# Two matmuls on the same high weights made one of 512 columns, in a split-precision block of two transformer layers

## The chip, the cores and the metric

The kernel runs on one core of a Trainium2 chip. The metric is the device time of one execution in microseconds (us), lower is better. Engines are called by their names in the profile: PE is TensorE (matmuls), PEld its weight loads, DVE VectorE, ACT ScalarE, POOL GpSimd, SP the engine that issues most DMAs.

## The reference

The input is a sequence of 256 tokens with 2048 channels in f32. Two blocks follow one another. The first: an RMS norm, one input projection, sliding-window attention with sinks, a state-space branch (convolution of four taps, chunked scan), gates, an output projection, a gated feed-forward layer with 5632 hidden channels and a gated side input. The second: a norm, sparse attention in three branches, a convolution of 31 taps, an output projection and a feed-forward layer whose hidden channels pass through a convolution of three taps. Nearly all work is dense projections; cut to its core:

```
proj = rmsnorm(h) @ w_in                              # 2048 x 10784
h = h + merged @ w_o                                  # 2048 x 2048
h = h + (silu(f @ w_gate) * (f @ w_up)) @ w_down      # 2048 x 5632, twice, and 5632 x 2048
...
u = causal_depthwise_conv_2(h @ w_up_2, cw, cb)       # 2048 x 11264
a, gate = split(u)
x = x + (silu(gate) * a) @ w_down_2                   # 5632 x 2048
```

## The kernel before

Activations are held transposed: 128 channels on the partitions, the 256 tokens along the row. Weights stream in from memory once. Both are f32, and each is split in two parts of the rounded matmul type (fp32r): a high part, rounded, and a low part, the difference. A product then is three matmuls: high weights with high activations, high weights with low activations, low weights with high activations. The text calls these three a triple.

The work is a list of **units** (`all_units`). A unit makes 256 output channels, as two halves `m` of 128, from `nk` tiles of 128 input channels (16 as a rule, 22 for the down projections, 8 for `w_attn_br` and `w_out_2`). Its result fills one of PSUM's eight banks, 256 tokens for each half. A unit's weights come in pieces (`subs`) of up to four k-tiles x 256 channels, 512 KB. For each piece SP fetches it into one of four buffers `RAW` (as soon as the low split of the piece that had the buffer is done), ACT writes the rounded copy `wh` (one of five buffers, free when the matmuls five pieces ago are done), DVE writes `wl = raw - wh`, and PE multiplies. `make_plan` lays down one order of steps for all engines: the splits run four pieces ahead of the matmuls (`LEAD`); after a unit's last piece its end (`evac`, functions `ev_...`) is put in, and side work (attention, convolutions, the state-space scan, sums of squares for the norms) is put in by lanes, a step after each piece. Each engine carries out its steps strictly in that order, with semaphores between engines.

At a unit's end DVE reads the bank and scales it by the norm's root (`rb`), or adds it to the residual `H` (`ev_h`, `ev_fin`); then ACT and DVE do what the layer asks for. `ev_g2` and `ev_u2`, for example, run a convolution of three taps: two ACT instructions for the first tap, four of DVE for the others. The bank goes back to PE when the first DVE instruction has read it (`EMPTIED`, `bank_free`). Units take banks in turn out of (0, 1, 2), or out of `wide`, banks 0 to 4, in the feed-forward layers; side work uses the others.

A unit in which activations are the stationary operand (`nat`: `ev_v`, `ev_dt`, `ev_gate`, `ev_v2`) has the same three products with roles changed. High and low activations of a k-tile lie side by side in one row of 512 (`Acts.hi` and `Acts.lo`).

Of the kernel before, what the change touches and what calls it, by code (L numbers as in the profile page):

```python
# [15 lines left out]
P = 128  # L16
# [85 lines left out]
class Unit:  # L102
    def __init__(self, w, row0, nk, c0, rhs, ev, i, nc=256, nat=False, gens=(), gens2=(), before=(), mid=(),
                 banks=(0, 1, 2), pace=1, hold=0, k0=0):
        self.w, self.row0, self.nk, self.c0, self.rhs, self.ev, self.i = w, row0, nk, c0, rhs, ev, i
        self.nc, self.nat, self.gens, self.gens2 = nc, nat, list(gens), list(gens2)
        self.before, self.mid, self.banks, self.pace, self.hold, self.k0 = before, mid, banks, pace, hold, k0
# [10 lines left out]
def all_units():  # L118
    us = []
    add = lambda *p, **k: us.append(Unit(*p, **k))  # L120
    for i in range(4):
        add("w_in", 0, 16, 256 * i, "U1", "ev_q", i, mid=(("norm", 0, 0),) if i == 0 else (), hold=2 if i == 0 else 0,
            gens=([stage("rotary", 0, 3), stage("biases", 0, 2)] if i == 0 else []) + [stage("rope_q", i, 2)])
    add("w_in", 0, 16, 1024, "U1", "ev_k", 0, gens=[stage("rope_k", 0, 2), stage("rope_k", 1, 2)])
# [3 lines left out]
    for i in range(12):  # L128
        add("w_in", 0, 16, 3584 + 256 * i, "U1", "ev_xbc", i, gens2=[stage("conv4", i, 3)])
    for i in range(8):  # L130
        add("w_in", 0, 16, 6688 + 256 * i, "U1", "ev_ga", i, before=("all",) if i == 0 else (),
            gens=[stage("ssd", g, 6) for g in range(4)] if i == 0 else (), pace=2)
        add("w_attn_br", 0, 8, 256 * i, "AT", "ev_oa", i, pace=2)
    for i in range(8):
        add("w_in", 0, 16, 1536 + 256 * i, "U1", "ev_z", i, before=("side",) if i == 0 else ())
    for i in range(8):
        add("w_in", 0, 16, 8736 + 256 * i, "U1", "ev_gs", i, mid=(("norm", 1, 0),) if i == 0 else (),
            hold=HOLD if i == 0 else 0)
    for i in range(8):
        add("w_ssd_br", 0, 16, 256 * i, "YH", "ev_os", i)  # L140
    for i in range(8):
        add("w_o", 0, 16, 256 * i, "MH", "ev_h", i)
    wide = (0, 1, 2, 3, 4)
    for half in range(2):
        for i in range(11):
            first = half == 0 and i == 0
            add("w_gate", 0, 16, 256 * (11 * half + i), "F1", "ev_g1", 11 * half + i, banks=wide,
                mid=(("norm", 2, 0),) if first else (), hold=HOLD if first else 0)
            add("w_up", 0, 16, 256 * (11 * half + i), "F1", "ev_u1", 11 * half + i, banks=wide)
        for i in range(8):  # L150
# [4 lines left out]
            add("w_down", 2816 * half, 22, 256 * i, "G1", "ev_h", 8 + 8 * half + i, banks=wide, k0=22 * half)  # L155
    for i in range(8):
        add("w_ple_gate", 0, 16, 256 * i, "P1H", "ev_pg", i, mid=(("norm", 3, 0),) if i == 0 else (),
# [32 lines left out]
    for i in range(8):  # L190
        add("w_out_2", 0, 8, 256 * i, "MXA", "ev_h", 24 + i, before=("side",) if i == 0 else ())
    for half in range(2):
        for i in range(11):
            first = half == 0 and i == 0
            add("w_up_2", 0, 16, FFN + 256 * (11 * half + i), "F2", "ev_g2", 11 * half + i, banks=wide,
                mid=(("norm", 5, 0),) if first else (), hold=HOLD if first else 0)
            add("w_up_2", 0, 16, 256 * (11 * half + i), "F2", "ev_u2", 11 * half + i, banks=wide)
        for i in range(8):
            add("w_down_2", 2816 * half, 22, 256 * i, "G2", "ev_h" if not half else "ev_fin",
                32 + i if not half else i, banks=wide, k0=22 * half)  # L200
    return us


def make_plan(us):


    plan, subs = [], []
    side, conv = Lane(plan), Lane(plan)
    for n, u in enumerate(us):
        k = 0  # L210
        while k < u.nk:
            subs.append((n, k, min(NSUB, u.nk - k)))
            k += NSUB
    turns, gb = [], 0
# [9 lines left out]
    for s, (n, k, c) in enumerate(subs):  # L224
# [10 lines left out]
        if k == 0:  # L235
# [10 lines left out]
            u.bank = u.banks[gb % len(u.banks)]  # L246
            gb += 1
        plan.append(("sub", s, 0))
        if k + c == u.nk:
# [27 lines left out]
def hybrid_block_kernel(nc, a, out):  # L277
    units = all_units()
    plan, subs = make_plan(units)

# [115 lines left out]

    def f32(ap):
# [53 lines left out]

    A = {"U1": Acts("u1", AHt, 0), "AT": Acts("at", BIGt, 0), "YH": Acts("yh", BIGt, 0), "MH": Acts("mh", AHt, 0),
# [10 lines left out]
    rk_pe, rk_d = steps("rope_k_pe"), steps("rope_k_d", "x", "y", "kd")  # L463
    evq_d, evk_d, evv_a = steps("ev_q"), steps("ev_k"), steps("ev_v", "c0", "c1")
# [17 lines left out]
    h_d = steps("h_added")  # L482
# [21 lines left out]
    for c in range(9):  # L504
# [13 lines left out]
    fin_d, res_d = steps("fin_added"), steps("result")  # L518


    EMPTIED = {"ev_q": (evq_d, None), "ev_k": (evk_d, None), "ev_v": (evv_a, "c1"), "ev_dt": (dt_d, "x1"),
               "ev_xbc": (evx_d, None), "ev_ga": (ga_d, None), "ev_oa": (oa_d, None), "ev_z": (z_d, "z"),
               "ev_gs": (gs_d, None), "ev_os": (os_d, "a"), "ev_h": (h_d, None), "ev_g1": (g1_d, "z"),
               "ev_u1": (u1_d, "u"), "ev_pp": (pp_a, None), "ev_pg": (pg_d, "a"), "ev_ca": (ca_d, None),
               "ev_cg": (cg_d, "a"), "ev_cmp": (cmp_d, "k"), "ev_k2": (k2_d, None), "ev_v2": (v2_a, "c1"),
               "ev_gate": (gt_d, "c1"), "ev_q2": (q2_d, None), "ev_add": (add_d, None), "ev_g2": (g2_d, "z"),
               "ev_u2": (u2_d, "z"), "ev_fin": (fin_d, None)}
# [1788 lines left out]
```

## Time and profile before

| | |
|---|---|
| median of 3 runs | 3062.24 us (3054.26 to 3065.12) |
| profiled execution | 3059.82 us, span 3058.0 us |
| mean granted clock of TensorE | 0.965 of full |
| PE busy | 2920.3 us (95%), 23840 matmuls and as many loads |
| DVE busy | 1892.8 us (62%) |
| ACT busy | 1345.3 us (44%) |
| read from memory | 489.56 MB, 161 GB/s over the span |

The span runs from the first to the last instruction of the profiled execution. Matmuls overlap in the pipeline, so the mean length of one (about 0.28 us) says little; what counts is the distance from one start to the next. In the timeline, neighbours of one kind are merged into one row with their count.

### The profile page before, as it was taken

How to read it: one execution, taken by the hardware profiler on the slowest of the kernel's cores; microseconds unless marked ns; L12 is line 12 of the kernel's file. 1: busy time of each engine (PE TensorE's matmuls, PEld its weight loads, DVE VectorE, ACT ScalarE, POOL GpSimd, SP SyncE). 2: the span in 40 equal slices, each digit the busy share in tenths (PEclk: the TensorE clock that was granted, in tenths of full speed). 3: DMA queues.
4: the chain of work that ended last, by engine and by line, in shares of the span. 5: the costliest groups of instructions: out<-in, count | busy, mean ns of one | idle time of the engine just before them, and what ended most of it. 6: DMA issues, size and time to landing. Idle time of an engine off the chain costs nothing.

```text
span 3058.0 us, 55192 instructions
## 1 busy us (share of the span) xinstructions
PE 2920.3 (95%) x23840; PEld 2874.3 (94%) x23840; DVE 1892.8 (62%) x2677; ACT 1345.3 (44%) x1922; POOL 9.8 (0%) x19
## 2 busy tenths in 40 slices
PE   7988998999999999999999989986999999999998
PEld 7978998999999999999999989975889999999998
DVE  5556755756665554555555747867667775477754
ACT  4245444543444443344444632344555444355442
POOL 0000000000000000000000000000000000000000
PEclk8999999999999999999999988887999999999998
DMA  6434553565556665666556464432345555655554
GB/s 198 122 98 123 166 152 111 183 181 185 182 174 188 184 183 178 186 187 185 180 180 194 155 173 123 138 97 62 102 141 172 186 180 183 189 180 179 188 181 128
DMA packets 495006, 495.26 MB, mean 162 GB/s; under 512 B 19818, under 2 KB 493371, under 8 KB 494731
## 3 DMA queue, kind: packets, MB, share of 16 engines
q1 hardware_dynamic: 491424, 484.11, 51.9%
q0 software_dynamic: 1376, 5.05, 0.6%
q8 instruction: 187, 3.06, 0.4%
q10 hardware_dynamic: 1964, 2.58, 0.2%
q14 instruction: 55, 0.45, 0.0%
HBM read 489.56 MB, written 2.12 MB: 161 GB/s over the span
## 4 chain that ended last, share of the span: by engine, by line
PE 83%; DVE 9%; ACT 4%; issue 2%; DMA 1%; SPq 0%; DVEq 0%; ACTq 0%
PE PS L615 82%; DVE wl L1439 3%; DVE CC L1447 2%; ACT wh L1004 1%; DMA raw<-in_w_in 1%; ACT SX2a L1004 1%; ACT SX2b L1004 1%; DVE TA L1447 0%; DVE SQA L1439 0%; ACT SX1b L1004 0%; ACT SX1a L1004 0%; DVE H L1447 0%; DVE TC L1447 0%; ACT TB L1004 0%; DVE Z L1439 0%
## 5 line engine op out<-in xcount | busy, mean ns | idle before, releaser
L1439 DVE TENSOR_TENSOR wl<-raw,wh 128x1024 fp32r<-128x1024 f32 (+2 forms) x944 | 1109.5, 1194 | 790.4 <-ACT wh L1004 789.8
L1004 ACT ACTIVATE wh<-raw 128x1024 fp32r<-128x1024 f32 (+2 forms) x944 | 953.5, 1029 | 818.0 <-PE PS L615 792.1
L615 PE MATMUL PS<-CHt,wh 128*128 128x256 f32 x5632 | 1014.2, 283 | 0.0
L615 PEld LDWEIGHTS PS<-CHt,wh 128*128 128x128 f32 x5632 | 878.6, 192 | 0.0
L615 PE MATMUL PS<-BIGt,wh 128*128 128x256 f32 x4608 | 851.1, 287 | 1.4 <-DVE TA L1439 0.9
L615 PE MATMUL PS<-CHt,wl 128*128 128x256 f32 x2816 | 796.9, 283 | 0.0
L615 PE MATMUL PS<-AHt,wh 128*128 128x256 f32 x4160 | 771.9, 288 | 23.2 <-DVE wl L1439 15.9
L615 PEld LDWEIGHTS PS<-BIGt,wh 128*128 128x128 f32 x4608 | 731.8, 195 | 8.4 <-issue 5.5
L615 PEld LDWEIGHTS PS<-AHt,wh 128*128 128x128 f32 x4160 | 660.8, 195 | 33.2 <-issue 17.7
L615 PE MATMUL PS<-BIGt,wl 128*128 128x256 f32 x2304 | 658.5, 286 | 0.0
L615 PE MATMUL PS<-AHt,wl 128*128 128x256 f32 x2080 | 594.7, 286 | 0.0
L615 PEld LDWEIGHTS PS<-CHt,wl 128*128 128x128 f32 x2816 | 540.7, 192 | 0.0
L615 PEld LDWEIGHTS PS<-BIGt,wl 128*128 128x128 f32 x2304 | 449.6, 195 | 0.0
L615 PEld LDWEIGHTS PS<-AHt,wl 128*128 128x128 f32 x2080 | 406.0, 195 | 0.0
L1447 DVE SCALAR_TENSOR_TENSOR CC<-Z,CV,CC 128x256 f32<-128x256 f32 x240 | 99.7, 482 | 0.0
L1439 DVE TENSOR_TENSOR Z<-PS,RB 128x512 f32<-128x512 f32 x86 | 59.4, 691 | 41.5 <-PE PS L615 41.4
L1004 ACT ACTIVATE BIGt<-TC 128x256 fp32r<-128x256 f32 x88 | 31.9, 409 | 120.3 <-DVE TC L1439 120.3
L1447 DVE SCALAR_TENSOR_TENSOR TA<-Z,CV,TA 128x256 f32<-128x256 f32 x160 | 69.2, 482 | 15.0 <-ACT TA L1004 14.7
L1004 ACT ACTIVATE TB<-TA 128x512 f32<-128x512 f32 x34 | 21.5, 631 | 78.5 <-DVE TA L1447 78.5
L1004 ACT ACTIVATE SX2a<-SX2a,SM 128x128 f32<-128x128 f32 x64 | 26.1, 443 | 60.0 <-DVE SM L2068 52.4
L1004 ACT ACTIVATE TA<-Z 128x512 f32<-128x512 f32 x30 | 19.0, 632 | 75.2 <-DVE Z L1439 75.2
L1439 DVE TENSOR_TENSOR H<-H,PS 128x512 f32<-128x512 f32 x56 | 38.3, 684 | 18.3 <-PE PS L615 18.2
(269 smaller groups left out, 1562.4 us busy)
## 6 DMA issues: line engine op xcount, KB each, us to landing
raw<-in_w_up SPq DMA_DIRECT2D x264, 512.0 KB, 4.5
raw<-in_w_in SPq DMA_DIRECT2D x240, 512.0 KB, 3.7
raw<-in_w_down SPq DMA_DIRECT2D x160, 512.0 KB, 3.7
raw<-in_w_gate SPq DMA_DIRECT2D x88, 512.0 KB, 4.6
raw<-in_w_ssd_br SPq DMA_DIRECT2D x32, 512.0 KB, 4.6
raw<-in_w_o SPq DMA_DIRECT2D x32, 512.0 KB, 4.6
raw<-in_w_ple_gate SPq DMA_DIRECT2D x32, 512.0 KB, 4.5
raw<-in_w_out SPq DMA_DIRECT2D x32, 512.0 KB, 3.6
```

Of the source, the lines that this page charges most:

```text
L615: return e.matmul(o, l, r, start=start, stop=stop, skip_group_check=True)
L1004: return e.activation(o, x, f, **k)
L1439: return e.tensor_tensor(o, x, y, op)
L1447: return e.scalar_tensor_tensor(out=o, in0=x, scalar=s, in1=y, op0=o0, op1=o1)
```

## The change

Units get a mode. "one" is as before. In the two new modes, "joint" and "turn", each half `m` of the unit gets a whole bank of its own: one matmul multiplies the high weights with the 512 columns of high and low activations (`both`) into the bank, another multiplies the low weights with the high activations into the bank's first 256 columns. The first 256 columns, the near half, then hold two of the three products, the last 256, the far half, the third. The two are added at the unit's end: ACT copies the far halves into the place of the result (`far_half`), DVE adds the near ones there (`join_halves`), and what followed reads that place instead of the bank. `ev_h` and `ev_fin` add near and far half to `H` one after the other.

A "joint" unit goes through its pieces as before; a "turn" unit does the whole of one half before the other, in pieces of eight k-tiles x 128 channels. The weights are laid out in memory beforehand by piece (`_stream`), so that each partition reads one run of 4 KB for a piece and not four of 1 KB. The changed units from `ev_z` on take banks 0 to 3, the earlier ones stay with 0 to 2. A pair of banks is returned to PE when `joined` says so.

These keep mode "one": the units with stationary activations, `ev_pp`, the 16 units of `w_in_2` with the activations U2, and the 8 of the second block's convolution half (`ev_add`, activations MXC).

```diff
+    order = lambda i: "turn" if i else "joint"
+    wide = (0, 1, 2, 3)
...
-        add("w_ssd_br", 0, 16, 256 * i, "YH", "ev_os", i)
+        add("w_ssd_br", 0, 16, 256 * i, "YH", "ev_os", i, mode=order(i), banks=wide)
...
+def pieces(us):
+    subs, gb, joins = [], 0, 0
+    for n, u in enumerate(us):
+        if u.mode != "one" and len(u.banks) % 2 == 0:
+            gb += gb % 2
+        b = u.banks[gb % len(u.banks)]
+        gb += 1
+        u.bank, u.turn = b, (0, 1)
+        if u.mode != "one":
+            b2 = u.banks[gb % len(u.banks)]
+            gb += 1
+            u.turn = (0, 1) if b < b2 else (1, 0)
+            u.pair = (min(b, b2), max(b, b2))
...
+        for ms in (((u.turn[0],), (u.turn[1],)) if u.mode == "turn" else ((0, 1),)):
+            step = NSUB * 2 // len(ms)
+            subs += [(n, ms, k, min(step, u.nk - k)) for k in range(0, u.nk, step)]
+    return subs
...
-            src = a[u.w][r0:r0 + c * P, u.c0:u.c0 + u.nc].rearrange("(t p) n -> p t n", p=P)
+            src = a[units[subs[s][0]].w][w_at[s]:w_at[s] + P * w].rearrange("(p f) -> p f", p=P)
...
+                if u.mode != "one":
+                    for j, m in enumerate(ms):
+                        o = PS[:, u.pair[m], :]
+                        mm(o, hi[:, t, j * P:(j + 1) * P], x.both(kt), firstk, False)
+                        tok = mm(o[:, 0:T], lo[:, t, j * P:(j + 1) * P], x.hi(kt), False, lastk)
...
+        def far_half(u, o):
+            e.wait_ge(sub_done.sem, u.end)
+            for m, x in far(u):
+                tok = af(o[:, m], x, ACT.Copy)
+            tok.then_inc(far_out.sem)
...
+        def join_halves(u, o):
+            e.wait_ge(far_out.sem, far_out.at(u.join))
+            for m, x in near(u):
+                tok = tt(o[:, m], x, o[:, m], ADD)
+            tok.then_inc(joined.sem)
+            e.wait_ge(joined.sem, joined.at(u.join))
...
         def ev_g2(n, u):
-            e.wait_ge(sub_done.sem, u.end)
-            tt(Z[0][:, :, 30:286], bank(u.bank), two(rb(0)), MUL).then_inc(g2_d.sem)
+            join_halves(u, z)
+            tt(z, z, two(rb(0)), MUL).then_inc(g2_d.sem)
...
-            tt(h, h, bank(u.bank), ADD).then_inc(h_d.sem)
+            tt(h, h, near(u)[0][1], ADD).then_inc(h_d.sem)
+            e.wait_ge(h_d.sem, h_d.at(i, "near"))
+            tt(h, h, far(u)[0][1], ADD).then_inc(h_d.sem)
```

`near(u)` and `far(u)` give both banks in one view where they are neighbours, and two views, one for each half, where they are not (0 and 2).

## Rows read from the trace of the kernel before

**Rows 1.** The page: engines' busy time (share) and instructions, the chain's costliest line

```profile
PE 2920.3 (95%) x23840; PEld 2874.3 (94%) x23840; DVE 1892.8 (62%) x2677; ACT 1345.3 (44%) x1922; POOL 9.8 (0%) x19
...
PE PS L615 82%; DVE wl L1439 3%; DVE CC L1447 2%; ACT wh L1004 1%; DMA raw<-in_w_in 1%; ACT SX2a L1004 1%; ACT SX2b L1004 1%; DVE TA L1447 0%; DVE SQA L1439 0%; ACT SX1b L1004 0%; ACT SX1a L1004 0%; DVE H L1447 0%; DVE TC L1447 0%; ACT TB L1004 0%; DVE Z L1439 0%
```

**Rows 2.** Stretches: length, busy us of each engine (instructions), clock, DMA share, GB/s

```profile
517.40:1761.20 1243.80, 1241.09 (x10309) 1240.40 (x10308) 726.68 (x799) 549.65 (x670) 2.05 (x4) 1.00 0.59 180
1761.20:2278.10 516.90, 447.36 (x3496) 421.91 (x3497) 356.41 (x749) 215.43 (x417) 6.10 (x8) 0.87 0.40 116
2278.10:2533.30 255.20, 255.20 (x2126) 255.10 (x2126) 181.85 (x241) 128.62 (x167) 0.00 (x0) 1.00 0.58 182
```

**Rows 3.** Waits of PE: us in total, times, longest

```profile
PE PS L742 <- ACT SX1a L1004: 15.0, 4, 5.6
...
PE PS L615 <- DVE SQA L1439: 9.9, 2, 7.6
```

**Rows 4.** Timeline of PE, dense stretch: start us, length us, instruction, count

```profile
1004.87 0.28 PE L615 MATMUL PS<-CHt,wl 128*128 128x256 f32 x1
...
1005.23 0.28 PE L615 MATMUL PS<-CHt,wl 128*128 128x256 f32 x1
```

**Rows 5.** The page's costliest groups: the low-weight matmuls, one for each triple

```profile
L615 PE MATMUL PS<-CHt,wl 128*128 128x256 f32 x2816 | 796.9, 283 | 0.0
...
L615 PE MATMUL PS<-BIGt,wl 128*128 128x256 f32 x2304 | 658.5, 286 | 0.0
L615 PE MATMUL PS<-AHt,wl 128*128 128x256 f32 x2080 | 594.7, 286 | 0.0
```

**Rows 6.** Timeline of PE, 32-column matmuls of ev_dt, at two clocks

```profile
109.01 0.26 PE L615 MATMUL PS<-wl,AHt 128*128 128x32 f32 x1
...
109.34 0.26 PE L615 MATMUL PS<-wl,AHt 128*128 128x32 f32 x1
...
118.07 0.59 PE L615 MATMUL PS<-wh,AHt 128*128 128x32 f32 x2
...
118.71 0.59 PE L615 MATMUL PS<-wh,AHt 128*128 128x32 f32 x2
```

**Rows 7.** Timeline of PE's weight loads, 512-column f32 matmuls

```profile
1805.98 0.19 PEld L615 LDWEIGHTS PS<-BMR,M 128*128 128x128 f32 x1 [0.24 <-issue]
...
1807.27 0.19 PEld L615 LDWEIGHTS PS<-BIGt,wh 128*128 128x128 f32 x1 [0.24 <-issue]
```

**Rows 8.** Timeline of PE, the first triples after other work

```profile
355.21 0.28 PE L615 MATMUL PS<-AHt,wl 128*128 128x256 f32 x1
...
356.04 0.40 PE L615 MATMUL PS<-AHt,wh 128*128 128x256 f32 x2
```

**Rows 9.** Groups by form: evacuations like the added ones (busy us, mean ns)

```profile
L1439 DVE TENSOR_TENSOR Z<-PS,RB 128x512 f32<-128x512 f32 x86 | 59.4, 691 | 41.5 <-PE PS L615 41.4
...
L1004 ACT ACTIVATE PR<-PS 128x512 f32<-128x512 f32 x8 | 4.7, 583 | 0.0
```

**Rows 10.** Timeline of DVE over two units, ev_u2 and then ev_g2

```profile
2372.33 0.69 DVE L1439 TENSOR_TENSOR Z<-PS,RB 128x512 f32<-128x512 f32 x1 [0.57 <-PE PS L615]
2373.69 1.77 DVE L1447 SCALAR_TENSOR_TENSOR TC<-Z,CV,TC 128x256 f32<-128x256 f32 x4 [0.67 <-ACT TC L1004]
2375.57 0.69 DVE L1439 TENSOR_TENSOR TC<-TC,TA 128x512 f32<-128x512 f32 x1
...
2378.01 3.50 DVE L1439 TENSOR_TENSOR wl<-raw,wh 128x1024 fp32r<-128x1024 f32 x3 [0.50 <-ACT wh L1004]
2382.05 1.23 DVE L1439 TENSOR_TENSOR wl<-raw,wh 128x1024 fp32r<-128x1024 f32 x1 [0.55 <-ACT wh L1004]
2383.85 0.69 DVE L1439 TENSOR_TENSOR Z<-PS,RB 128x512 f32<-128x512 f32 x1 [0.57 <-PE PS L615]
...
2388.63 3.50 DVE L1439 TENSOR_TENSOR wl<-raw,wh 128x1024 fp32r<-128x1024 f32 x3 [0.26 <-ACT wh L1004]
```

**Rows 11.** The page's DMA issues: count, KB each, median us to landing

```profile
raw<-in_w_up SPq DMA_DIRECT2D x264, 512.0 KB, 4.5
```

More of the change, by code:

```diff
@@ L190, in all_units @@
     for i in range(8):
-        add("w_out_2", 0, 8, 256 * i, "MXA", "ev_h", 24 + i, before=("side",) if i == 0 else ())
+        add("w_out_2", 0, 8, 256 * i, "MXA", "ev_h", 24 + i, mode="turn", banks=wide, before=("side",) if i == 0 else ())
     for half in range(2):
@@ L194, in all_units, with weight_places @@
             first = half == 0 and i == 0
-            add("w_up_2", 0, 16, FFN + 256 * (11 * half + i), "F2", "ev_g2", 11 * half + i, banks=wide,
+            add("w_up_2", 0, 16, FFN + 256 * (11 * half + i), "F2", "ev_g2", 11 * half + i, banks=wide, mode=order(11 * half + i),
                 mid=(("norm", 5, 0),) if first else (), hold=HOLD if first else 0)
-            add("w_up_2", 0, 16, 256 * (11 * half + i), "F2", "ev_u2", 11 * half + i, banks=wide)
+            add("w_up_2", 0, 16, 256 * (11 * half + i), "F2", "ev_u2", 11 * half + i, banks=wide, mode="turn")
         for i in range(8):
             add("w_down_2", 2816 * half, 22, 256 * i, "G2", "ev_h" if not half else "ev_fin",
-                32 + i if not half else i, banks=wide, k0=22 * half)
+                32 + i if not half else i, banks=wide, k0=22 * half, mode=order(i))
     return us
+def pieces(us):
[11 more added lines that the diff above has]
+            u.pair = (min(b, b2), max(b, b2))
+            u.bank = None
+            u.join = None
+            if u.ev not in ("ev_h", "ev_fin"):
+                u.join = joins
+                joins += 1
+        for ms in (((u.turn[0],), (u.turn[1],)) if u.mode == "turn" else ((0, 1),)):
+            step = NSUB * 2 // len(ms)
+            subs += [(n, ms, k, min(step, u.nk - k)) for k in range(0, u.nk, step)]
+    return subs
+def weight_places(us, subs):
+    at, size = [], {}
+    for n, ms, k, c in subs:
+        u = us[n]
+        at.append(size.get(u.w, 0))
+        size[u.w] = at[-1] + P * c * (u.nc if len(ms) == 2 else P)
+    return at, size
 def make_plan(us):
-    plan, subs = [], []
+    plan = []
+    subs = pieces(us)
     side, conv = Lane(plan), Lane(plan)
[L209 to L214, printed above, removed]
     for s in range(NRAW):
@@ L245, in make_plan @@
                     side.width = what
-            u.bank = u.banks[gb % len(u.banks)]
-            gb += 1
         plan.append(("sub", s, 0))
-        if k + c == u.nk:
+        if k + c == u.nk and (len(ms) == 2 or ms[0] == u.turn[1]):
             u.end = s + 1
@@ L395, in bank, with tiles, near, far @@
         return PS[:, b, :].rearrange("p (m t) -> p m t", m=2)
+    def tiles(u, c0):
+        lo, hi = u.pair
+        if hi == lo + 1:
+            return [(slice(0, 2), PS[:, lo:hi + 1, c0:c0 + T])]
+        return [(slice(m, m + 1), PS[:, u.pair[m]:u.pair[m] + 1, c0:c0 + T]) for m in range(2)]
+    def near(u):
+        return tiles(u, 0)
+    def far(u):
+        return tiles(u, T)
+    def words(s):
+        n, ms, k, c = subs[s]
+        return c * (units[n].nc if len(ms) == 2 else P)
     def f32(ap):
@@ L517, in hybrid_block_kernel @@
     u2_a = steps("up2_a", "t00", "t01")
[L518 to L527, printed above, removed]
+    fin_d, res_d = steps("fin_added", "near", "far"), steps("result")
+    EMPTIED = {"ev_v": (evv_a, "c1"), "ev_dt": (dt_d, "x1"), "ev_h": (h_d, None), "ev_pp": (pp_a, None),
+               "ev_ca": (ca_d, None), "ev_cg": (cg_d, "a"), "ev_cmp": (cmp_d, "k"), "ev_k2": (k2_d, None),
+               "ev_v2": (v2_a, "c1"), "ev_gate": (gt_d, "c1"), "ev_q2": (q2_d, None), "ev_add": (add_d, None),
+               "ev_fin": (fin_d, None)}
     ends = {(u.ev, u.i): u.end for u in units}
@@ L2272, in _constants, with _stream @@
     return mats, mask1, oh, ohc.reshape(33, -1), invf[i % 32][:, None]
+def _stream(x):
+    us = all_units()
+    subs = pieces(us)
+    at, size = weight_places(us, subs)
+    flat = {w: np.empty(s, np.float32) for w, s in size.items()}
+    for (n, ms, k, c), o in zip(subs, at):
+        u = us[n]
+        c0, nc = (u.c0, u.nc) if len(ms) == 2 else (u.c0 + ms[0] * P, P)
+        r0 = u.row0 + k * P
+        piece = x[u.w][0][r0:r0 + c * P, c0:c0 + nc]
+        flat[u.w][o:o + piece.size].reshape(P, c, nc)[:] = piece.reshape(c, P, nc).transpose(1, 0, 2)
+    return flat
 def kernel(**inputs):
```

270 lines of the change are left out of this document (159 added, 111 removed).

## The prediction

> **What bounds the kernel now.** I read the page first. TensorE is busy 95% of the 3058.0 us span, VectorE 62%, ScalarE 44%, and the chain that ended last is 82% the matmuls of line 615 [rows 1]. The table by stretch says where that holds: from 517.4 to 1761.2 us and from 2278.1 us nearly to the end TensorE has no gap, while in the attention, convolution and state-space stretches (up to 517.4 us, and 1761.2 to 2278.1 us) it stands idle for 13% of the time in the longest [rows 2], for softmax steps and sums of the other engines among others [rows 3]. DMA is at 0.59 of its engines in the dense stretches [rows 2]. So in the dense stretches the time is a number of matmuls times the distance between their starts. That distance is read from the timeline: a triple (high weights on high activations, high on low, low on high), each 256 columns, repeats every 0.36 us, 120 ns a matmul [rows 4]. The columns alone take 256/2.4 = 106.7 ns at the full clock; 13.3 ns of each 120 belong to the matmul as such. The whole question is whose 13.3 ns these are.
>
> **What the change does to TensorE.** The units in the new modes hold all triples but those of the 16 unchanged U2 units (32 triples each) and of the 8 MXC units (16 each): 2816 + 2304 + 2080 triples [rows 5], less 512 and 128, is 6560. Of them 5504 lie in the dense stretches (z, gs, os: 768; w_o 256; both gate/up pairs 2816; both downs 1408; ple gate 256) and 1056 before 517.4 us or in the 8 MXA units. In each, two 256-column matmuls become one of 512 columns. The columns stay 768, so only the fixed part of one matmul and one weight load can go.
>
> No row shows a 512-column matmul of this rounded type, so I bound it. The nearest rows:
> - With 32 columns, matmul and load repeat in 0.33 us per triple, 111 to 112 ns each, at the full clock [rows 6]. The load of 128 weight columns alone takes that, and a 256-column matmul (106.7 ns) just covers it. The low weights' load will lie behind 512 columns for nothing; the next high weights' load lies behind the 256-column matmul as now, so that one stays at 120 ns.
> - The plain f32 matmul of 512 columns starts its loads from 1805.98 to 1807.27 in three steps, 430 ns each [rows 7]. That is two 2.4 GHz cycles a column, 426.7 ns, and 3 ns of fixed part. When the load is well hidden, hardly anything is left. Lower bound for the new matmul: 213.3 + 3 = 216 ns.
> - If the 13.3 ns are a fixed part of any matmul of this type, whatever its load does: 213.3 + 13.3 = 226.7 ns.
> - If they are a slower stream (120/256 ns a column): 240 ns, and nothing is gained at all.
>
> After other work on TensorE the first seven distances are shorter, 355.21 to 356.04, 119 ns each [rows 8]; a stream that needed the 120 ns would not do that, but a load and a matmul that have to fall into step might. That speaks against the last and leaves the first two, which are 11 ns apart. The f32 row has the same stream length and load, the 120 ns row the same type; I see no row that is nearer and take the middle, 221.5 ns. A pair is then 341.5 ns for 360: 18.5 ns saved, with 24 and 13.3 as ends (and 0 for the slower stream).
>
> One rule speaks against the change: in the Trainium skill, TensorE: Matmul & The Clock Gate, section "Back-to-back issue gap", a warm matmul takes N/2.4 + 2.5 ns, so a matmul less would save 2.5 ns. By it the sum would be 6560 x 2.5 = 16 us, and the present triple 327 ns; this trace has 360 ns [rows 4], so here the rule misses 11 ns a matmul, though it would fit the f32 row.
>
> At half the clock the triple takes 0.64 us (118.07 to 118.71) [rows 6], which is 768 columns at 1.2 GHz exactly: there nothing is saved. The dense stretches are granted 1.00 [rows 2].
>
> Dense: 5504 x 18.5 = 102 us. Elsewhere: 1056 x 18.5 = 20 us, of which I keep half, 10 us, since TensorE there waits for chains that don't get shorter [rows 3], and some of such stretches runs at half the clock (0.87 on the mean in the longest) [rows 2].
>
> **What it adds.** Of the 201 changed units, 153 get a ScalarE copy of the far half (as PR<-PS, 0.58 us) and a VectorE add (as Z<-PS,RB, 0.69 us); the 48 ev_h and ev_fin units add to H twice where they added once, taken at the same 0.69 us [rows 9]. That is 153 x 0.58 = 89 us on ScalarE and 201 x 0.69 = 139 us on VectorE. Both have room on average: 1345 + 89 and 1893 + 139 in some 2950 us. On ScalarE the copy waits for the unit's end, but what is queued behind it, the split of piece s+5, waits for the same piece anyway (NHL is 5). On VectorE the split of s+5 stands behind the join; TensorE wants that split four pieces (some 11 us) later, so a join that is 1.4 us longer is covered.
>
> The tight place is the second gate/up pair, where VectorE is busy 182 of 255 us [rows 2]. Its turn for two units [rows 10]: 5.68 us from the Z of ev_u2 to the next split (2372.33 to 2378.01), 4.78 us for ev_g2 (2383.85 to 2388.63), eight splits 2 x (3.50 + 1.23) = 9.46 us; with two joins at 0.69 + 0.11 (the gap between dependent instructions there, 2375.46 to 2375.57) 21.5 us. TensorE will take 64 x 0.3415 = 21.9 us for these two units. So it fits by 2%, as long as the far copies run while VectorE is still splitting; if not, 0.58 us and a hand-over come on top for each unit, and the stretch is VectorE's, at 23 us, about what it takes now (23.04).
>
> Banks: with (0, 1, 2) the second half of a unit wants the first bank of the unit before. That leaves half a unit, 5.5 us, for copy and add (1.3 us, or 1.6 where the two banks aren't neighbours and each becomes two instructions); but for ev_oa, with 8 k-tiles, only 2.7 us, beside the state-space work on both engines. Between 0 and 1 us for each of 8: I take 4 us in all. With four banks a pair comes round after a whole unit: no wait. The end of the kernel and the MXA stage, where sums of squares are awaited [rows 3], get one add later each: 1.6 us.
>
> The DMA moves the same bytes, as rows of 4 KB for 1 KB; at 0.59, a pace 5% faster means 0.62. A piece lands 4.5 us after its issue [rows 11], and four of them are on the way while TensorE takes 2.73 us for each, so I put the new layout at nothing. Without those four buffers each piece would be late by 4.5 - 2.73 = 1.8 us at most.
>
> **Sum.** 3059.8 us (the profiled run: span 3058.0 and 1.8 around it) - 102 - 10 + 4 + 1.6 = 2953. The median of the runs, 3062.2, is 2.4 above the profiled one: 2956 us.
>
> **Rivals.**
> - The load is all of it, and the new matmul takes 216 ns. For it: the f32 row [rows 7]. Against: f32 reads a column in twice the time, so it need not show what this type needs. 24 x 5504 = 132, 24 x 528 = 13: 2923 us. VectorE's 21.5 us in the tight place then equals TensorE's 64 x 0.336.
> - The cost is per column (237 to 240 ns), and the merge gives 0 to 3 ns: -17 to 0, and 6 added: 3050 to 3068 us. For it: 120 ns to the nanosecond in long runs [rows 4]. Against: the shorter distances of [rows 8]. The rule named above would end at the same place, 3050.
> - The evacuations take it back: the far copy isn't hidden, VectorE sets the pace in the tight place, and joins late in the three-bank stages stop TensorE. At 23 us a pair the 22 pairs lose their 26 us gain: 2980; it decides for slower only where the pair takes 23.04 + 76/22 = 26.5 us, for which nothing is in sight.
> - Slower: the whole-bank matmul streams worse than two halves, from 240 ns up. At the plain f32 rate of 430 ns [rows 7] it would be 190 x 6560 = 1246 us longer, 4300 us. Against: the present 256 columns in 120 ns are already faster than that rate.
>
> **Chances.** Fixed part between the bounds (2930 to 2990): 0.48, with its own range 2925 to 2992 from 24 and 13.3 ns. Load alone: 0.22. Per column: 0.16, a fifth of it slower. Evacuations: 0.10, half faster, the rest split. Slower stream: 0.04. What can be told from no change is 0.5%, 15 us, so faster is under 3047: 0.48 + 0.22 + 0.03 + 0.05 = 0.78; same 0.13; slower 0.09. The range runs from below the load-alone case, 2915, up into the evacuation and per-column cases, 3035.
>
> **What would show it.** In a dense stretch the timeline should alternate high and low matmuls with a pair every 0.336 to 0.347 us; 0.36 would be the per-column case. Line 615 should count some 6560 matmuls and loads fewer. In the gate/up stretches new ScalarE copies from PS of 0.58 us and VectorE adds of 0.69 us; the second pair shorter by as much as the first, else VectorE binds there. Waits of PE on VectorE adds should be a few us, in the ga/oa stretch. DMA packets should fall to about a quarter, without effect. A pair distance outside 0.336 to 0.347, or TensorE idle in the gate/up stretches, would make the number wrong.

## The result, and the profile after

The changed kernel takes 3036.95 us (median of 5 runs, 3031.45 to 3049.39), beside 3058.49 us for the kernel before in the same comparison (5 runs, 3054.26 to 3065.12): a ratio of 0.9936, interval 0.9908 to 0.9963. It is faster, by 21.5 us or 0.6%; the forecast was 2956 us, 81 us lower, and its range ended at 3035. The profiled run took 3036.66 us, its span is 3034.9 us, 23.1 us less than before.

From the page of the changed kernel: busy time of the engines, the weights' DMA queue, and the groups that answer to the parts of the change.

```profile
PE 2876.1 (95%) x17280; PEld 2523.5 (83%) x17280; DVE 2020.3 (67%) x2889; ACT 1422.6 (47%) x2086; POOL 9.8 (0%) x19
...
q1 hardware_dynamic: 139168, 484.11, 48.1%
...
L671 PE MATMUL PS<-CHt,wh 128*128 128x512 f32 x2816 | 986.8, 396 | 1.2 <-DVE wl L1580 1.2
...
L1073 ACT ACTIVATE Z<-PS 128x512 f32<-128x512 f32 (+1 forms) x90 | 51.4, 576 | 113.2 <-PE PS L671 113.1
...
L1580 DVE TENSOR_TENSOR Z<-PS,Z 128x512 f32<-128x512 f32 (+1 forms) x90 | 59.6, 666 | 52.7 <-ACT Z L1073 51.7
```

The work changed as planned: 23840 - 17280 = 6560 matmuls fewer, far copies of 0.58 us, joins of 0.67 us; VectorE has 127.5 us more work and ScalarE 77.3 us more [rows 1]. So the surprise is not in how much work there is.

The changed kernel by stretches: until the first gate unit beside the state-space work (355.4 us) and the first z unit (537.3 us), the first dense stretch, the middle, the second dense stretch to the last matmul. The columns are those of [rows 2].

```profile
0.00:355.40 355.40, 302.50 (x1664) 259.76 (x1665) 217.28 (x382) 153.74 (x283) 1.67 (x8) 0.89 0.40 133
355.40:537.30 181.90, 168.43 (x1085) 144.66 (x1084) 120.53 (x168) 90.75 (x158) 0.00 (x0) 0.96 0.42 139
537.30:1761.80 1224.50, 1219.17 (x6921) 1058.13 (x6917) 785.43 (x895) 587.33 (x745) 1.81 (x3) 1.00 0.55 182
1761.80:2280.30 518.50, 447.54 (x3369) 415.98 (x3370) 361.82 (x758) 214.88 (x417) 6.35 (x8) 0.87 0.38 116
2280.30:3022.80 742.50, 738.15 (x4250) 644.75 (x4248) 526.68 (x672) 375.43 (x484) 0.00 (x0) 1.00 0.55 184
...
2280.30:2528.20 247.90, 246.66 (x1423) 215.28 (x1422) 198.19 (x267) 140.78 (x191) 0.00 (x0) 1.00 0.54 187
```

And the same view of the kernel before, for its second dense stretch to the last matmul, which [rows 2] does not hold whole:

```profile
2278.20:3045.90 767.70, 765.37 (x6361) 764.72 (x6360) 484.88 (x606) 351.95 (x437) 0.00 (x0) 1.00 0.56 177
```

The first dense stretch is 1243.8 - 1224.5 = 19.3 us shorter [rows 2], the second 767.7 - 742.5 = 25.2: 45 us, where 102 had been forecast. And the first dense stretch begins some 20 us later than before (537.3 for 517.4 us), where a small gain had been forecast. Two questions, then: why a pair gives so little, and what the first 537 us lose.

The pair itself, from the changed kernel's timeline of PE, in the first and in the second dense stretch (start us, length us, instruction):

```profile
1004.72 0.40 PE L671 MATMUL PS<-CHt,wh 128*128 128x512 f32 x1
1004.95 0.28 PE L671 MATMUL PS<-CHt,wl 128*128 128x256 f32 x1
1005.07 0.40 PE L671 MATMUL PS<-CHt,wh 128*128 128x512 f32 x1
...
1006.84 0.40 PE L671 MATMUL PS<-CHt,wh 128*128 128x512 f32 x1
...
2317.34 0.47 PE L671 MATMUL PS<-CHt,wh 128*128 128x512 f32 x1 [1.24 <-DVE wl L1580]
...
2699.79 0.40 PE L671 MATMUL PS<-CHt,wh 128*128 128x512 f32 x1
...
2701.87 0.40 PE L671 MATMUL PS<-CHt,wh 128*128 128x512 f32 x1
```

Six pairs take 1006.84 - 1004.72 = 2.12 us, 353.3 ns each; later six take 2701.87 - 2699.79 = 2.08 us, 346.7 ns. These are two steady rhythms. Read along the timeline, the first holds from the z units to the end of the first downs, the second nearly all the way from 2317 us, where TensorE had just waited, to the end. Neither is 341.5, and against the 360 ns of [rows 4] they save 6.7 and 13.3 ns, not 18.5.

What PE waits for until 540 us, in the form of [rows 3]:

```profile
PE PS L813 <- ACT SX1a L1073: 19.2, 4, 6.4
...
PE PS L813 <- ACT SX1b L1073: 10.5, 4, 3.0
...
PE PS L671 <- DVE QT L1580: 3.6, 1, 3.6
PE PS L671 <- DVE TA L1580: 3.4, 1, 3.4
```

The wait for SX1a has grown from 15.0 [rows 3] to 19.2 us, and there are waits for QT and TA, whose joins empty banks. All in all TensorE is idle for 537.3 - 302.5 - 168.4 = 66.4 us of these stretches, 15 us more than before (the rows of before stand with e3). That leaves some 5 us, and what brings the 15 is open too; experiments have to say it.

### The profile page after: what moved, and what is told of

Its sections match the earlier page's. It is cut to its first block, busy times and chain, and to the rows that moved or that the text cites. A ratio compares the mean times of both kernels' runs of the same rounds, so it can differ in the third digit from the quotient of the medians.

```text
span 3034.9 us, 42699 instructions
## 1 busy us (share of the span) xinstructions
PE 2876.1 (95%) x17280; PEld 2523.5 (83%) x17280; DVE 2020.3 (67%) x2889; ACT 1422.6 (47%) x2086; POOL 9.8 (0%) x19
## 3 DMA queue, kind: packets, MB, share of 16 engines
HBM read 489.56 MB, written 2.12 MB: 162 GB/s over the span
## 4 chain that ended last, share of the span: by engine, by line
PE 78%; DVE 13%; ACT 5%; issue 2%; DMA 1%; ACTq 0%; DVEq 0%
PE PS L671 78%; DVE wl L1580 4%; DVE CC L1588 2%; ACT wh L1073 2%; DVE TA L1588 1%; ACT SX2a L1073 1%; DVE Z L1580 1%; ACT SX2b L1073 1%; DVE TC L1588 1%; DMA raw<-in_w_in 1%; DVE SQA L1580 0%; DVE TA L1580 0%; ACT SX1b L1073 0%; ACT SX1a L1073 0%; DVE H L1588 0%
## 5 line engine op out<-in xcount | busy, mean ns | idle before, releaser
L1580 DVE TENSOR_TENSOR wl<-raw,wh 128x1024 fp32r<-128x1024 f32 (+3 forms) x944 | 1098.9, 1192 | 593.2 <-ACT wh L1073 591.9
L1073 ACT ACTIVATE wh<-raw 128x1024 fp32r<-128x1024 f32 (+3 forms) x944 | 943.6, 1028 | 586.2 <-PE PS L671 557.1
L671 PE MATMUL PS<-CHt,wh 128*128 128x512 f32 x2816 | 986.8, 396 | 1.2 <-DVE wl L1580 1.2
L671 PE MATMUL PS<-BIGt,wh 128*128 128x512 f32 (+1 forms) x2816 | 837.2, 363 | 4.3 <-DVE TA L1580 3.4
L671 PE MATMUL PS<-AHt,wh 128*128 128x512 f32 (+1 forms) x2208 | 762.6, 395 | 30.4 <-DVE wl L1580 17.5
L671 PEld LDWEIGHTS PS<-CHt,wh 128*128 128x128 f32 x2816 | 528.6, 188 | 129.3 <-issue 1.5
L671 PEld LDWEIGHTS PS<-BIGt,wh 128*128 128x128 f32 x2816 | 510.8, 195 | 93.3 <-issue 7.4
L671 PEld LDWEIGHTS PS<-AHt,wh 128*128 128x128 f32 x2208 | 417.7, 194 | 132.5 <-issue 20.3
L1073 ACT ACTIVATE Z<-PS 128x512 f32<-128x512 f32 (+1 forms) x90 | 51.4, 576 | 113.2 <-PE PS L671 113.1
L1580 DVE TENSOR_TENSOR Z<-PS,Z 128x512 f32<-128x512 f32 (+1 forms) x90 | 59.6, 666 | 52.7 <-ACT Z L1073 51.7
L1580 DVE TENSOR_TENSOR Z<-Z,RB 128x512 f32<-128x512 f32 x86 | 59.6, 692 | 2.9
L1073 ACT ACTIVATE TB<-TA 128x512 f32<-128x512 f32 x34 | 21.5, 633 | 81.2 <-DVE TA L1588 81.1
```

The source lines that it names most:

```text
L671: return e.matmul(o, l, r, start=start, stop=stop, skip_group_check=True)
L1073: return e.activation(o, x, f, **k)
L1580: return e.tensor_tensor(o, x, y, op)
```

## Experiments

Times of before, measured beside them on the same chip: 3059.65 us (e1 to e4), 3057.93 (e5 to e8), 3059.36 (e9, e10), 3064.41 (e11, e12, one run), 3056.68 (e13).

**What does a matmul of 512 columns cost?** e1 gives the low matmul 512 columns as well, so that all are alike.

```diff
-  tok = mm(o[:, 0:T], lo[:, t, j * P:(j + 1) * P], x.hi(kt), False, lastk)
+  tok = mm(o, lo[:, t, j * P:(j + 1) * P], x.both(kt), False, lastk)
```

> The low weights multiply 512 columns too (the far half then also holds low times low, which the reference's product has anyway), so each pair is two 512-column matmuls, and each load lies behind 512 columns. Theory A, a stream that is slower than a column a cycle, with phases that settle at 0.44 to 0.47 ns a column: a pair takes 460 to 472 ns in the dense stretches, and the total grows by 5504 x 110 to 120 ns, to about 3680 us. Theory B, a fixed 13 ns for each matmul: 453 ns, 3600 us. Theory C, the load is what is slow, and it shows only where 256 columns cover it: 432 to 440 ns, 3510 to 3550 us.

One run: 3655.57 us. Its timeline of PE:

```profile
1000.02 0.39 PE L671 MATMUL PS<-AHt,wh 128*128 128x512 f32 x1
...
1002.29 0.39 PE L671 MATMUL PS<-AHt,wh 128*128 128x512 f32 x1
```

Ten matmuls in 2.27 us, 227 ns each, a pair in 0.453 to 0.454 us and the same throughout: 213.3 + 13.3 = 226.7 ns is met, the ranges of A and C are not. The 13.3 ns stand at 512 columns as at 256, and a load that lies behind 512 columns doesn't take them away. The total is 56 us above the 3600 of Theory B; 41 of them lie outside the dense stretches, 33 before the z units and 8 in the middle. (The Trainium skill, TensorE: Matmul & The Clock Gate, section "Back-to-back issue gap", gives N/2.4 + 2.5 ns for the gap of an isolated warm matmul, from which 512 columns are estimated at 215.8 ns; this run has 11 ns more.)

**Does the other traffic slow TensorE?** e2 loads and splits only the first five pieces and uses them over and over, so that hardly any DMA and hardly any split runs beside the matmuls.

```diff
-  if kind != "fetch":
+  if kind != "fetch" or s >= NHL:
       continue
...
-  e.wait_ge(split_lo.sem, s + 1)
+  e.wait_ge(split_lo.sem, min(s + 1, NHL))
...
   def split(s, _):                          (both splits)
+    if s >= NHL:
+        return
```

> Weights are fetched and split for the first five pieces only and then used again for all (the rest of the weights is left out, the output is not the reference's); ScalarE, VectorE and DMA lose the splits and fetches, the matmuls and their order stay. Theory A/B, the slow 512-column matmul is TensorE's own: pairs of 346.7 or 353.3 ns in the dense stretches as in the changed kernel, and a total within 20 us of 3037. Theory D, the memory traffic of the splits and fetches slows TensorE's reading: pairs fall to 336 to 341 ns, the dense stretches by 60 to 90 us.

One run: 2910.8 us. Timeline of PE at the two places shown above, and one stretch of its table:

```profile
999.73 0.40 PE L671 MATMUL PS<-CHt,wh 128*128 128x512 f32 x1
...
1001.85 0.40 PE L671 MATMUL PS<-CHt,wh 128*128 128x512 f32 x1
...
2699.76 0.40 PE L671 MATMUL PS<-CHt,wh 128*128 128x512 f32 x1
...
2701.88 0.40 PE L671 MATMUL PS<-CHt,wh 128*128 128x512 f32 x1
```

```profile
303.90:480.70 176.80, 168.22 (x1085) 144.10 (x1084) 63.95 (x119) 43.19 (x109) 0.00 (x0) 0.97 0.00 1
```

2.12 us for six pairs at both places: 353.3 ns with DMA at 1 GB/s. Traffic is not what slows the pairs, nor is 346.7 a property of the second gate/up pair. The total fell by 126 us, where at most 20 had been expected, and not by the pairs: the state-space stretch ends at 480.7 instead of 537.3 us, and the middle takes 448.4 us instead of 518.5. There the work that this run leaves out sets the time; whether it is the splits on ScalarE and VectorE or the fetches it can't say, since both are gone.

**What do the added evacuations cost?** e3 keeps the banks, copies and adds of the change, but issues two 256-column matmuls for the one of 512.

```diff
-  mm(o, hi[:, t, j * P:(j + 1) * P], x.both(kt), firstk, False)
+  mm(o[:, 0:T], hi[:, t, j * P:(j + 1) * P], x.hi(kt), firstk, False)
+  mm(o[:, T:2 * T], hi[:, t, j * P:(j + 1) * P], x.lo(kt), False, False)
```

> The changed kernel with its banks, evacuations and layout, but the high weights multiply high and low activations in two 256-column matmuls again, 360 ns a triple. Theory: the added evacuations and the tighter banks cost 18 to 22 us before 517 us of the kernel before and next to nothing later: 3058 + 20 = 3078 us, first stretches up to the state-space end 537 to 540 us, dense stretches as before. Rival: the loss of the first stretches comes from the faster pieces (side work has fewer us to hide behind), then this one is at 3058 to 3063 us.

3083.33 us (3081.53 to 3086.6), ratio 1.0083 [1.0058, 1.0109]. By stretch:

```profile
0.00:356.20 356.20, 304.17 (x2241) 291.25 (x2242) 217.43 (x382) 153.57 (x283) 1.67 (x8) 0.90 0.42 133
356.20:539.00 182.80, 171.88 (x1437) 164.42 (x1436) 120.43 (x168) 90.77 (x158) 0.00 (x0) 0.96 0.44 139
539.00:1783.80 1244.80, 1241.21 (x10313) 1240.01 (x10310) 785.17 (x895) 587.91 (x745) 1.80 (x3) 1.00 0.56 180
```

The evacuations and banks alone cost 24 us, and nearly all of it before 539 us; the dense stretch has the 1244 us of before [rows 2], with 58 us more on VectorE. The 512-column matmul by itself is therefore worth 3083.3 - 3037.0 = 46 us, 7 ns a triple, and nearly nothing of it falls before the z units (539.0 against 537.3 us).

The same two stretches of the kernel before:

```profile
0.00:339.50 339.50, 298.26 (x2240) 286.44 (x2241) 205.26 (x359) 145.28 (x260) 1.67 (x8) 0.91 0.48 139
339.50:517.00 177.50, 167.35 (x1437) 160.41 (x1436) 110.93 (x147) 82.53 (x137) 0.00 (x0) 0.99 0.49 143
```

TensorE is idle for 51.4 of these 517.0 us, and for 63.0 of e3's 539.0. The same matmuls (e3 has one more record) keep it busy for 465.6 us before and for 476.1 in e3, at a lower granted clock: 0.90 and 0.96 on the mean, for 0.91 and 0.99. So of the 22 us some 12 are longer waits and 10 are slower matmuls. That the added waits bring the clock down is argued here, from the stops of e11 below, and not tested by itself.

e4 asks it the other way: the units of the first stretches (q, k, xbc, ga, oa) as before the change, all others changed.

```diff
-  add("w_in", 0, 16, 3584 + 256 * i, "U1", "ev_xbc", i, mode="turn", ...)
+  add("w_in", 0, 16, 3584 + 256 * i, "U1", "ev_xbc", i, ...)
...
-  join_halves(u, z)
-  tt(z, z, two(rb(0)), MUL).then_inc(evx_d.sem)
+  e.wait_ge(sub_done.sem, u.end)
+  tt(z, bank(u.bank), two(rb(0)), MUL).then_inc(evx_d.sem)
```

> The units of q, k, xbc, ga and oa as in the kernel before (mode one, three banks, no added evacuation), all others as changed. Theory, the added evacuations and bank waits cost there what was lost: the end of the state-space stretch is back at 517 to 520 us and the total is 3037 - 18 = 3019 us, ratio to the kernel before 0.987. Rival, the loss was slow states of the matmul distance and of the clock: 3030 to 3037 us.

3010.71 us (3007.34 to 3012.04), ratio 0.984 [0.9819, 0.9862]: 26 us better than the whole change, of which 22 lie before the z units (515.3 for 537.3 us); the rest lies in stretches that the edit doesn't touch.

```profile
0.00:338.50 338.50, 297.13 (x2241) 285.37 (x2242) 205.15 (x359) 145.06 (x260) 1.67 (x8) 0.92 0.43 140
338.50:515.30 176.80, 168.74 (x1438) 161.49 (x1436) 110.79 (x147) 82.43 (x137) 0.00 (x0) 0.98 0.44 143
515.30:1737.50 1222.20, 1218.07 (x6922) 1058.13 (x6917) 785.16 (x895) 586.95 (x745) 1.80 (x3) 1.00 0.56 183
```

Two things could do that: a bank that comes free later (Theory K), or the longer queues (Theory E). e9 gives the first units one bank each as before, but keeps the copy and the add.

```diff
-  add("w_in", 0, 16, 3584 + 256 * i, "U1", "ev_xbc", i, mode="turn", ...)
+  add("w_in", 0, 16, 3584 + 256 * i, "U1", "ev_xbc", i, mode="solo", ...)
...
+  if u.mode == "solo":
+      return [(slice(0, 2), bank(u.bank))]
```

> The first units (q, k, xbc, ga, oa) keep three 256-column matmuls into one bank, as in the kernel before, so a bank is wanted again only two units later; but their ends keep the added work, a ScalarE copy of the bank and a VectorE add of the bank to the copy ahead of the scaling (these units' results are doubled by it, so the output is not the reference's). All other units as changed. Theory E, the added work in the two engines' queues costs the first stretches their 20 us: the state-space stretch ends at 533 to 538 us and the total is 3028 to 3037 us. Theory K, the late return of the two banks costs them: 517 to 520 us and 3010 to 3015 us.

3033.18 us (3026.15 to 3045.08), ratio 0.9914 [0.9889, 0.9938].

```profile
0.00:350.70 350.70, 304.43 (x2241) 292.00 (x2242) 214.29 (x370) 152.64 (x276) 1.67 (x8) 0.89 0.41 133
350.70:534.20 183.50, 171.84 (x1438) 164.38 (x1436) 122.77 (x170) 90.93 (x154) 0.00 (x0) 0.96 0.43 141
```

With three matmuls a triple in these units it is to be compared with e3: 534.2 for 539.0 us. So 17 of the 22 us remain when the banks are as before, and with them the low granted clock (0.89 and 0.96; e4, without the added work, has 0.92 and 0.98). Banks and the order of pieces, which e9 gives up together, are worth 5 us at most, as much as e4, e7, e10 and e13, whose first units are alike, differ among themselves (515.3 to 520.1 us). Theory K falls: the added work in the two queues, with the waits and the clock that follow it, is the main cost.

The profiled run of e9 is its slowest, 3045.08 us, and shows what a rhythm is worth. The change has the same units in the second dense stretch, but here the pairs ran at 353.3 ns from its gate/up pair to the end, and the stretch took 13 us longer than the 742.5 us above:

```profile
2275.30:3031.20 755.90, 751.55 (x4250) 651.48 (x4248) 527.23 (x672) 375.68 (x484) 0.00 (x0) 1.00 0.55 180
```

So the total of a kernel with alternating pairs depends on which rhythm a run takes. Whether that is why the five runs of the change spread over 18 us isn't shown, since one of them has a trace.

e8 leaves the kernel of before as it is and only lays its weights out by piece.

```diff
-  src = a[u.w][r0:r0 + c * P, u.c0:u.c0 + u.nc].rearrange("(t p) n -> p t n", p=P)
+  src = a[u.w][w_at[s]:w_at[s] + P * f].rearrange("(p f) -> p f", p=P)
```

> The kernel before with nothing changed but the weights' place in memory, by piece, one run of 4 KB for each partition. Theory: the transfers were hidden, 3058 us within 5 us, with packets down to some 130,000 and the DMA share a little lower. Rival: shorter landings help the first pieces and the stretch ends, 3 to 10 us less.

3055.97 us (10 runs, 3048.03 to 3060.16), ratio 0.999 [0.998, 1.0], with this line on its page, where the kernel before has 491424 packets and 51.9%:

```profile
q1 hardware_dynamic: 139168, 484.11, 49.8%
```

**Does the alternation of lengths cost something?** 226.7 + 120 is 346.7 ns; 353.3 is 6.7 more. e5 puts two high matmuls and then two low ones, e6 all eight high ones of a piece and then its low ones, so that unlike neighbours are rarer.

```diff
+  for kt in (k + t, k + t + 1):
+      mm(o, hi[:, kt - k, cut], x.both(kt), kt == 0, False)
+  for kt in (k + t, k + t + 1):
+      tok = mm(o[:, 0:T], lo[:, kt - k, cut], x.hi(kt), False, kt == u.nk - 1)
```

> The changed kernel with the order of matmuls high, high, low, low over two k-tiles instead of high, low, high, low; the same matmuls, loads and results. The run with 512-column low matmuls gave 226.7 ns for each, so the fixed part is 13.3 ns, and two highs and two lows should take 2 x 226.7 + 2 x 120 = 693.3 ns. Theory L: the 353.3 ns pairs of the changed kernel are a rhythm into which alternating lengths of stream and load fall; with another order it goes or takes another value, and where it goes (693.3 ns for two pairs everywhere in the dense stretches) the total is 3037 - 22 = 3015 us. Rival P: the 6.7 ns belong to each matmul of 512 columns that follows one of 256 (or to its load); then each two pairs still hold one such change and take 700 ns, total 3026 us.

> The changed kernel with all high matmuls of a piece's half (eight, or four in joint units) ahead of its low ones; the same matmuls, loads and results. Both theories expect equal neighbours to take 226.7 and 120 ns; theory L expects 346.7 ns a pair on the mean in all dense stretches, total 3037 - 22 = 3015 us; rival P one change of 6.7 ns in eight pairs, 3018 us. If pairs stay at 353.3 ns, the extra belongs to neither.

e5: 3017.77 us (3016.85 to 3019.42), ratio 0.9872 [0.9857, 0.9887]. e6: 3021.37 us (3019.79 to 3025.71), 0.9885 [0.9871, 0.99]. Timelines of PE, e5 and then e6; neighbours of one kind stand in one row with their count:

```profile
1005.23 0.62 PE L671 MATMUL PS<-CHt,wh 128*128 128x512 f32 x2
...
1008.02 0.63 PE L671 MATMUL PS<-CHt,wh 128*128 128x512 f32 x2
```

```profile
1006.34 2.00 PE L671 MATMUL PS<-CHt,wh 128*128 128x512 f32 x8
...
1009.13 2.00 PE L671 MATMUL PS<-CHt,wh 128*128 128x512 f32 x8
```

Eight pairs in 2.79 us, 349 ns a pair, in both. That is 4.6 ns better than 353.3, and still not 346.7, in e6 too, where only one neighbour in eight is of another length. So a fixed price for each change of length isn't the explanation.

e7 and e10 put the better order on top of e4 (e7 the order of e6, e10 that of e5).

> The first units (q, k, xbc, ga, oa) as in the kernel before, and in the others all highs of a piece's half ahead of its lows: the two edits together. If both act by themselves, 3011 - 22 = 2989 us, ratio 0.977 to the kernel before.

> The first units as in the kernel before, the others in the order high, high, low, low. If both edits act by themselves, 3011 - 19 = 2992 us; where the rhythm of the first run of either kind is by chance the better one already, up to 3003 us. Ratio to the kernel before 0.978 to 0.982.

e7: 3003.47 us (3002.38 to 3008.94), 0.9829 [0.9812, 0.9845]. e10: 3003.55 us (2999.72 to 3004.86), 0.9809 [0.9794, 0.9824]. Expected were 2989 us for e7 and 2992, or up to 3003, for e10. Two stretches of e10:

```profile
517.40:1725.60 1208.20, 1203.18 (x6922) 1050.62 (x6919) 785.41 (x895) 587.43 (x745) 1.82 (x4) 1.00 0.56 185
1725.60:2245.10 519.50, 446.12 (x3369) 414.69 (x3370) 361.33 (x756) 214.14 (x416) 6.34 (x8) 0.88 0.36 116
```

The first dense stretch gains the 14 us (1222.2 to 1208.2), but the middle one, which the order hardly touches, took 519.5 us and in e4 1737.5 to 2250.9, 513.4 us. What moves the middle stretch by a few us stays open. In the second dense stretch, where e4 already ran at 346.7 ns, the new order at 349 loses 2 us (744.9 for 742.5).

**What sets the rhythm?** e11 lets TensorE stop at 44 places of the gate/up units; e12 puts one 32-column matmul there instead.

```diff
+  at = k == 0 and 0 in ms and u.mode != "one" and u.ev in ("ev_g1", "ev_u1", "ev_g2", "ev_u2") and u.i % 2 == 1
-  e.wait_ge(split_lo.sem, s + 1)
+  e.wait_ge(split_lo.sem, s + (5 if at else 1))                               (e11)
+  if at:                                                                      (e12)
+      mm(PS[:, u.pair[0], 0:32], hi[:, 0, 0:P], x.hi(k)[:, 0:32], True, True)
```

> In 44 places of the two gate/up pairs TensorE waits until the splits are five pieces ahead, so that it stands still for some 2 to 3 us and then goes on with the same pairs. In the changed kernel the pair distance was 353.3 ns through the whole first gate/up pair and 346.7 ns through the second after one pause at 2315.8 us. Theory R, a rhythm is taken when TensorE starts again after a pause and is kept until the next: both distances appear in both gate/up pairs, each section with one of them from its first pairs to its end. Theory S, the rhythm belongs to the stage (its tiles, its banks, its place in the program): 353.3 in every section of the first, 346.7 in every section of the second. Theory T, the rhythm has to do with the work of the other engines or the DMA: the distance changes inside sections. The time is about 44 x 2.5 = 110 us above 3037 by all three, near 3145.

> At the same 44 places one 32-column matmul of the same weights is put ahead of the first matmul of a bank, which then overwrites what it wrote; TensorE doesn't stop there. If only a pause sets the rhythm anew: 353.3 ns in the whole first gate/up pair, as in the changed kernel, and one rhythm from the pause at some 2316 us on. If any neighbour of another length does it (Theory U): sections of both distances between the short matmuls, in both gate/up pairs. Theory S: 353.3 in the first, 346.7 in the second. The time: 44 x 0.11 = 5 us above 3037, and by Theory U up to some 10 us less, where sections fall to 346.7: 3030 to 3045.

e11, one run: 3414.74 us, far above the 3145 expected, since most stops were 5 to 9 us long (two about 3, one 12.5) and not 2.5, and TensorE came back at half the clock, 1.2 GHz, after 43 of the 44 (a pair in 0.64 us at 1187 us). From its timeline, two sections, with the stop between them:

```profile
1173.21 0.39 PE L671 MATMUL PS<-CHt,wh 128*128 128x512 f32 x1
...
1175.29 0.39 PE L671 MATMUL PS<-CHt,wh 128*128 128x512 f32 x1
...
1187.22 0.77 PE L671 MATMUL PS<-CHt,wh 128*128 128x512 f32 x1 [5.18 <-DVE wl L1581]
...
1199.77 0.40 PE L671 MATMUL PS<-CHt,wh 128*128 128x512 f32 x1
...
1201.89 0.40 PE L671 MATMUL PS<-CHt,wh 128*128 128x512 f32 x1
```

2.08 us for six pairs before the stop, 2.12 after it. Of the 44 sections that begin with a stop, 24 ran at 346.7 and 20 at 353.3 ns (13 and 9 in the first gate/up pair, 11 and 11 in the second), each from its first pairs at full clock to its end within the gate/up pair. Theories S and T fall; R holds.

e12, one run: 3025.14 us, 5 us under the range expected. Timeline of PE around the second of its short matmuls (the row "x2" is the 32-column matmul with the next high one):

```profile
933.64 0.40 PE L671 MATMUL PS<-CHt,wh 128*128 128x512 f32 x1
...
935.76 0.40 PE L671 MATMUL PS<-CHt,wh 128*128 128x512 f32 x1
...
936.11 0.50 PE L671 MATMUL PS<-CHt,wh 128*128 128x32 f32 x2
...
936.57 0.40 PE L671 MATMUL PS<-CHt,wh 128*128 128x512 f32 x1
...
938.30 0.39 PE L671 MATMUL PS<-CHt,wh 128*128 128x512 f32 x1
```

2.12 us for six pairs ahead of it, 1.73 us for five behind it, 346 ns: no stop is needed, a short neighbour can do it too (Theory U). The short matmul before it, at 924.7 us, had left the pairs at 353.3. e13 uses that, on the kernel of e4, with a short matmul ahead of the second and fourth unit of each merged stage.

> The kernel of e4 (first units as before the change), with one 32-column matmul ahead of the second and the fourth unit of each merged stage, some two dozen in all, 3 us of TensorE. Theory U, now with what e12 showed (a matmul of another length takes the pairs from 353.3 to 346.7 ns, and they stay there until the stage ends): e4's profiled run held some 3,290 pairs at 353.3 ns and 2,310 at 346.7; of the 3,290 some 3,000 come down by 6.67 ns, 20 us, less 3: near 2994 us, between 2990 and 3000, and 346.7 through the first gate/up pair. If the rhythm is drawn by chance and e12 was one draw: both distances in the first gate/up pair, and 3000 to 3014 us, as e4 (3010.7 us).

3001.68 us (2996.88 to 3003.06), ratio 0.9814 [0.98, 0.9827]: 9 us under e4. That is 2 us above the range of Theory U, and within the 3000 to 3014 of its rival, a draw by chance.

```profile
520.10:1729.10 1209.00, 1204.87 (x6940) 1059.12 (x6936) 785.44 (x895) 587.66 (x745) 1.81 (x3) 1.00 0.55 185
```

The first dense stretch is 13 us shorter than e4's, and its gate/up pair ran at 346.7 ns but for some 15 pairs: at 898 us TensorE's matmuls for the sums of squares came between, and the pairs after them took 353.3 ns, until the next short matmul at 905.7. In e12 and e13 together, by the timelines: where a short matmul met pairs at 346.7 ns, they stayed there, 57 of 57 times; where it met 353.3, it brought 346.7 in 7 of 14 cases (one short matmul of the 72 met neither). So a short matmul is a draw that goes one way only; other work, as the sums of squares here and at 587 us of e2, can bring the longer rhythm back. Some 920 pairs stayed at 353.3 instead of e4's 3,290, so (3,290 - 920) x 6.67 ns = 16 us came back, less 3 us for the short matmuls; the z units began 5 us later than in e4, which is the rest of the difference. Its median is the lowest, but e7, e10 and e13 can't be told apart.

## Why the prediction was wrong

The direction was right, the size was not. Its terms, one by one:

- **The new matmul's length** ("take the middle, 221.5 ns"): mis-sized. The upper bound was the truth, 226.7 ns (e1). The step that failed is the argument from the plain f32 rows [rows 7], a stream at another rate, which pulled the value away from the type's own 13.3 ns [rows 4]. The shorter distances of [rows 8], read as a load and a matmul falling into step, said nothing on this. Price: 5.2 ns x 5504 = 29 us.
- **The low matmul stays at 120 ns**: right for a pair of 346.7 ns, but a pair of unlike lengths can also lock to 353.3 ns, a rhythm that no row of before shows, where all lengths are equal. The 3392 dense triples of the first dense stretch (z, gs, os, w_o, gate/up, downs, ple gate) ran mostly so: 6.7 ns x 3392 = 23 us. With both, the first stretch's 3392 x 18.5 = 63 us come down to 22, and the second's 2112 x 18.5 = 39 to 28. Measured are 19.3 and 25.2; some 3 us in each stay unexplained. A pair outside 0.336 to 0.347 us was the prediction's own sign of being wrong, and it showed.
- **Elsewhere, half of 20 us kept**: wrong. Up to the z units the merge gave 1.7 us (e3 against the change): TensorE was busy for 5 us less, and idle for 3 us more.
- **What it adds, 5.6 us** (4 for banks, 1.6 for later adds): wrong in size and in kind. It was 24 us (e3), nearly all of it before the z units. The 4 us for banks may even be right (5 at most, e9); the rest is the copies and adds in the queues of ScalarE and VectorE, as longer waits of TensorE and as matmuls at a lower granted clock (12 and 10 us, e3), which the prediction had at nothing. The prediction read room "on average" off the page and looked for the tight place in a dense stretch; but in the stretches where TensorE waits for softmax, convolution and state-space steps [rows 2, 3], a copy and an add stand in the queues of the very engines that it waits for. This was its own rival ("the evacuations take it back"), placed in the wrong stretch.
- **The tight place** in the second gate/up pair held: VectorE 198.2 of 247.9 us, TensorE busy for 246.7. That stretch came down by 7.3 us, from 255.2 [rows 2].
- **Half the clock**: the prediction read 0.64 us a triple off [rows 6] as 768 columns at 1.2 GHz. The matmuls there have 32 columns, so these rows don't show it. What it concluded holds: in the trace of before three 256-column matmuls take 0.63 to 0.64 us at half the clock (14.59 to 15.22 us), and so does a pair in e11.
- **The layout at nothing**: right, by e8, with packets at 28% of before. **Traffic**: no part in it, by e2.
- **The rival "per column"** (3050 to 3068 us) came near the time with the wrong reason: a matmul of 512 columns is not slower per column, as e1's 226.7 ns shows. The ends of the forecast range left out that several smaller errors could add up. With 226.7 ns alone the forecast would have been some 2985 us, still far too low.

The sum as measured: 19.3 + 25.2 us gained in the dense stretches, 20 lost before them, 1.6 in the middle; 22.9 of the 23.1 us by which the span is shorter.

What stays open is why pairs of unlike lengths have two rhythms, and what decides which one a start takes; shown is that the choice is made where something interrupts the pairs, that it is kept until the next interruption, and that the shorter one outlasted every 32-column matmul.

## What to carry to other kernels

Undo such a change where the engine waits for side chains: there added evacuations cost time, however low the average load. Here 33 of them, some 41 us of work on two engines, cost 22 us, and leaving those units alone gave as much back. Before a price is taken from a row of another type, put the disputed instruction alone in a long uniform run: e1 settled in one run what 11 ns of bounds left open. And when instructions of different lengths alternate, read the distance over several pairs and at several places: two rhythms 2% apart hid in one trace, and one stretch took 13 us more or less by them.

## What was not expected of the hardware

- For this rounded type the distance of uniform matmuls is their columns at 2.4 GHz plus 13.3 ns, at 256 columns (120 ns, [rows 4]) and at 512 (226.7 ns, e1) alike.
- Alternating 512 and 256 columns locks to 346.7 or 353.3 ns a pair for over a thousand pairs on end, with traffic (the changed kernel) or without (e2); 24 of 44 starts after a stop drew the shorter one (e11), and a 32-column matmul moved the longer to the shorter in 7 of 14 cases and never back (e12, e13). Matmuls for sums of squares between the pairs did bring the longer back (587 us of e2, 898 us of e13).
- After 43 of 44 stops, most of them 5 to 9 us long, TensorE came back at half the clock (1.2 GHz), 0.64 us a pair; over 900 to 1700 us of e11 the granted clock was 0.92 on the mean.
